# Second, casting transfer for the rounded part of each weight piece, in place of ScalarE's rounding

## What is computed

```python
for l in range(DEPTH):
    h = h + 0.5 * swiglu(rmsnorm(h, ffn1_norm[l]), ffn1_w_gu[l], ffn1_w_down[l])
    h = h + mixer(rmsnorm(h, mix_norm[l]), w_in[l], ret_gn[l], w_ret_proj[l],
                  w_sb_proj[l], w_out[l], pos, valid)
    h = h + 0.5 * swiglu(rmsnorm(h, ffn2_norm[l]), ffn2_w_gu[l], ffn2_w_down[l])
```

## Time and profile before

| what | value |
|---|---|
| median of 3 runs | 1291.62 us (1291.59 to 1291.71) |
| the profiled execution, whole | 1291.65 us |
| its span, first to last instruction | 1289.8 us |
| granted TensorE clock, mean | 0.999 |
| weight transfers on SP's queue | 407 of 512 KB and two halves |
| read from HBM | 217.04 MB, 169 GB/s over the span |

### The profile page before, as it was taken

How to read it: one execution, slowest core, us unless ns; L and a number is a source line. 1 busy time by engine, 2 the same in 40 slices (tenths; PEclk the granted TensorE clock), 3 DMA queues, 4 the chain that set the end, 5 groups by cost and what they waited for, 6 DMA issues and landing times.

```text
span 1289.8 us, 26118 instructions
## 1 busy us (share of the span) xinstructions
PE 1281.2 (99%) x10298; PEld 1276.1 (99%) x10298; DVE 866.0 (67%) x1078; ACT 697.2 (54%) x932; POOL 54.2 (4%) x48
## 2 busy tenths in 40 slices
PE   8999999999999999999999999999999999999998
PEld 8999999999999999999999999999999999999998
DVE  7766556878876776665476665568788777766653
ACT  6544445757766554444454444457578665544442
POOL 2000001000000010000010000010000000100000
PEclk9999999999999999999999999999999999999999
DMA  7655554544344455555545555555544445555552
GB/s 293 198 178 178 178 169 160 180 166 146 118 142 144 160 187 178 167 179 180 172 157 194 170 171 180 176 168 180 166 145 131 138 158 179 196 185 182 187 179 83
DMA packets 60705, 219.30 MB, mean 170 GB/s; under 512 B 6864, under 2 KB 6992, under 8 KB 60496
## 3 DMA queue, kind: packets, MB, share of 16 engines
q1 hardware_dynamic: 60048, 217.01, 50.6%
q10 hardware_dynamic: 576, 1.11, 0.3%
HBM read 217.04 MB, written 1.05 MB: 169 GB/s over the span
## 4 chain that ended last, share of the span: by engine, by line
PE 98%; DVE 1%; ACT 1%; DMA 0%; issue 0%; ACTq 0%
PE bank L1102 31%; PE bank L1104 31%; PE bank L1103 31%; PE bank L1246 1%; PE bank L1337 1%; PE bank L1366 1%; PE bank L1235 1%; PE bank L1218 0%; DMA raw<-stream 0%; PE bank L1253 0%; PE bank L1057 0%; PE bank L1116 0%; DVE w_lo L656 0%; PE bank L1061 0%; PE bank L1059 0%; PE bank L1236 0%
## 5 line engine op out<-in xcount | busy, mean ns | idle before, releaser
L656 DVE TENSOR_TENSOR w_lo<-raw,w_hi 128x1024 fp32r<-128x1024 f32 x407 | 508.8, 1256 | 270.5 <-ACT w_hi L406 265.7
L1102 PE MATMUL bank<-xh,w_hi 128*128 128x272 f32 (+1 forms) x2224 | 642.6, 289 | 0.1
L406 ACT ACTIVATE w_hi<-raw 128x1024 fp32r<-128x1024 f32 x407 | 428.3, 1058 | 391.8 <-PE bank L1104 391.0
L1104 PE MATMUL bank<-xh,w_lo 128*128 128x272 f32 (+1 forms) x2224 | 635.8, 286 | 0.0
L1103 PE MATMUL bank<-xl,w_hi 128*128 128x272 f32 (+1 forms) x2224 | 635.5, 286 | 0.0
L1103 PEld LDWEIGHTS bank<-xl,w_hi 128*128 128x128 f32 x2224 | 418.6, 188 | 0.2
L1102 PEld LDWEIGHTS bank<-xh,w_hi 128*128 128x128 f32 x2224 | 418.3, 188 | 0.5 <-DVE w_lo L656 0.3
L1104 PEld LDWEIGHTS bank<-xh,w_lo 128*128 128x128 f32 x2224 | 418.1, 188 | 0.0
L1104 PE MATMUL bank<-gh,w_lo 128*128 128x272 f32 (+1 forms) x1016 | 290.9, 286 | 0.0
L1102 PE MATMUL bank<-gh,w_hi 128*128 128x272 f32 (+1 forms) x1016 | 290.7, 286 | 0.0
L1103 PE MATMUL bank<-gl,w_hi 128*128 128x272 f32 (+1 forms) x1016 | 289.8, 285 | 0.0
(11 more groups left out here) (197 smaller groups left out, 731.3 us busy)
## 6 DMA issues: line engine op xcount, KB each, us to landing
raw<-stream SPq DMA_DIRECT2D x407, 512.0 KB, 3.3
table<-tables SPq DMA_DIRECT2D x1, 1424.0 KB, 7.8
gain_h<-tokens SPq DMA_DIRECT2D x2, 272.0 KB, 6.2
raw<-stream SPq DMA_DIRECT2D x2, 256.0 KB, 4.5
out<-rv_gb ACTq DMA_DIRECT2D x2, 256.0 KB, 2.8
out<-rv_gb SPq DMA_DIRECT2D x2, 256.0 KB, 2.7
rv_gb<-squares SPq DMA_DIRECT2D x1, 384.0 KB, 8.0
gain_h<-tokens ACTq DMA_DIRECT2D x1, 300.0 KB, 4.2
```

The lines of the kernel that those rows point to most:

```text
L406: eng.activation(w_hi[:, slot, :], raw[:, slot, :], ACT.Copy).then_inc(hi_ready, 1)
L656: eng.tensor_tensor(w_lo[:, slot, :], raw[:, slot, :], w_hi[:, slot, :].bitcast(F32), ALU.subtract).then_inc(lo_ready, 1)
L1102: pe.matmul(out, wh, hi, start=first, stop=False)
L1104: mm = pe.matmul(out, wl, hi, start=False, stop=last)
```

## The change

Pieces 4 to 407 get their w_hi by a second transfer of the same 512 KB from HBM, which casts from float32 to fp32r on the way. POOL's queue issues it (`cast_hi`), after a wait for the piece that used the slot before. ACT's roundings of these pieces go away; those of the first four stay. DVE's `split_lo` now waits for both transfers of its piece. POOL's additions and copies are placed at fixed steps between the issues: POOL's program has the same loops as the others. In the rotary part, where ACT relied on split_hi's wait, it now has one of its own.

```diff
+        hi_in = [sem(f"hi_in{i}") for i in range(RING)]
...
+            def cast_hi(n, slot):
+
+                pool.wait_ge(piece_done, n - (RING - 1))
+                pool.dma_start(w_hi[:, slot, :], stream[n]).then_inc(hi_in[slot], 16)
+
+            def squares_after(rnd, p):
+
+                if p:
+                    add_squares(rnd, p)
+                if p == PAIRS - 1:
+                    join_squares(rnd)
+
+            def join_squares(rnd):
+                pool.wait_ge(ssq_added, rnd * ADDS + ADDS)
+                pool.tensor_tensor(ssq[:, 0, :], ssq[:, 0, :], ssq[:, 1, :], ALU.add).then_inc(ssq_joined, 1)
+
+            def ffn(l, f):
...
+                for j in range(4):
+                    cast_hi(base + (j + RING), (off + j) % RING)
+                    if base == 0 and j < ADDS:
+                        add_squares(0, j + 1)
...
+                with pool.Fori(1, ITERS) as it:
+                    for j in range(4):
+                        cast_hi(base + it * 4 + (j + RING), (off + j) % RING)
+                for q in range(QUADS):
+                    for c in range(ITERS):
+                        s = GU + q * ITERS + c
+                        if not last or s + RING < FFN:
+                            cast_hi(base + (s + RING), (off + s) % RING)
+                        if c >= ITERS - 2 and not last:
+                            squares_after(l * 3 + 2 * f + 1, 2 * q + c - (ITERS - 2))
+
+            def mixer(l):
+                base = l * PER_LAYER + FFN
+                for s in range(MIX):
+                    cast_hi(base + (s + RING), (FFN + s) % RING)
+                    if s == 2 * U_V + 1:
+                        place_first_keys(l)
+                    if s == 2 * U_SK + 4:
+                        place_second_keys(l)
+                    if s == 2 * U_SQ[1] + 1:
+                        place_last_queries(l)
+                    if s >= S_OUT and s % 2:
+                        squares_after(l * 3 + 2, (s - S_OUT) // 2)
...
                 with eng.Fori(1, ITERS) as it:
-                    for j in range(4):
-                        split_hi(base + it * 4 + (j + RING), (off + j) % RING)
-                        if j == 1:
-                            silu(it)
+                    silu(it)
                     hidden_hi(it)
...
                     if s % 2 and u < U_V:
 
                         q0 = first_kept(u, qf)
+                        eng.wait_ge(piece_done, base + (s + 1))
...
-            def split_lo(n, slot):
-
-                eng.wait_ge(hi_ready, n + 1)
+            def split_lo(n, slot, first=False):
+
+                if first:
+                    eng.wait_ge(hi_ready, n + 1)
+                else:
+                    eng.wait_ge(hi_in[slot], (n - slot) * (16 // RING))
+                    eng.wait_ge(raw_ready[slot], (n - slot) * (16 // RING) + 16)
                 eng.tensor_tensor(w_lo[:, slot, :], raw[:, slot, :], w_hi[:, slot, :].bitcast(F32),
                                   ALU.subtract).then_inc(lo_ready, 1)
```

More of the change, by code:

```diff
@@ L350, in add_squares @@
                 pool.tensor_tensor(ssq[:, :, :], ssq[:, :, :], squares_home(rnd, p), ALU.add).then_inc(ssq_added, 1)
-            def layer(l):
[L353 to L359, removed]
+            def cast_hi(n, slot):
+                pool.wait_ge(piece_done, n - (RING - 1))
+                pool.dma_start(w_hi[:, slot, :], stream[n]).then_inc(hi_in[slot], 16)
@@ new lines, in squares_after @@
+            def squares_after(rnd, p):
[7 more added lines that the diff above has]
+            def ffn(l, f):
+                off = 0 if f == 0 else FFN + MIX
+                base = l * PER_LAYER + off
+                last = first_query(l) > 0 and f == 1
+                for j in range(4):
+                    cast_hi(base + (j + RING), (off + j) % RING)
+                    if base == 0 and j < ADDS:
+                        add_squares(0, j + 1)
+                if base == 0:
+                    join_squares(0)
+                with pool.Fori(1, ITERS) as it:
[8 more added lines that the diff above has]
+                            squares_after(l * 3 + 2 * f + 1, 2 * q + c - (ITERS - 2))
@@ L361, in place_keys @@
+            def layer(l):
+                ffn(l, 0)
+                mixer(l)
+                ffn(l, 1)
             def place_keys(keys):
@@ L369, in place_tail_queries, with place_first_keys @@
                 mm.then_inc(placed, 1)
-            def place_queries(l):
+            def place_first_keys(l):
                 pool.wait_ge(ssum_done, l * 3 + 2)
@@ L377, in place_queries, with place_second_keys @@
                 pool.wait_ge(rq_tail_in, l + 1)
+            def place_second_keys(l):
                 pool.wait_ge(ret_tail_scores, l + 1)
@@ L381, in place_queries, with place_last_queries @@
                 pool.wait_ge(key_tail_ready, 2 * l + 2)
+            def place_last_queries(l):
                 pool.wait_ge(unit_evicted, evicted(l, U_SQ[1]))
@@ L399, in raw_count, with split_hi @@
                 return (n - slot) * (16 // RING) + 16
-            def split_hi(n, slot, first=False):
-                if not first:
-                    eng.wait_ge(piece_done, n - (RING - 1))
+            def split_hi(n, slot):
                 eng.wait_ge(raw_ready[slot], raw_count(n, slot))
@@ L456, in ffn @@
                         eng.preload_act_table_set("silu_and_others")
-                    split_hi(base + (j + RING), (off + j) % RING)
                 silu(0)
@@ L471, in ffn @@
                             take_h(l * 3 + 2 * f + 1, 2 * q + c - (ITERS - 2), q0, final=last)
-                        if not last or s + RING < FFN:
-                            split_hi(base + (s + RING), (off + s) % RING)
             def mixer(l):
@@ L480, in mixer @@
                         take_h(l * 3 + 2, (s - S_OUT) // 2, qf)
-                    split_hi(base + (s + RING), (FFN + s) % RING)
                     u = s // 2
@@ L628, in _ @@
             hi_of_h(0, 1, 0)
-            split_hi(1, 1, first=True)
+            split_hi(1, 1)
             eng.wait_ge(h_loaded[2], 16)
@@ L633, in _ @@
             hi_of_h(0, 3, 0)
-            split_hi(2, 2, first=True)
+            split_hi(2, 2)
             squares_of_h(0, 0, 0)
             squares_of_h(0, 1, 0)
-            split_hi(3, 3, first=True)
+            split_hi(3, 3)
             squares_of_h(0, 2, 0)
@@ L1016, in _ @@
             lo_of_h(0, 1, 0)
-            split_lo(1, 1)
+            split_lo(1, 1, first=True)
             eng.wait_ge(h_loaded[2], 16)
@@ L1021, in _ @@
             lo_of_h(0, 3, 0)
-            split_lo(2, 2)
-            split_lo(3, 3)
+            split_lo(2, 2, first=True)
+            split_lo(3, 3, first=True)
             eng.wait_ge(squares_in, 32)
```

## The result

The changed kernel takes 1525.97 us (median of 4 runs, 1520.25 to 1533.02), the one before 1291.63: 234 us more, a ratio of 1.182 (95% interval 1.179 to 1.185). The direction was forecast, and so was what happens in retention and stick-breaking. The size was not: the forecast was 97 us more, and 1526 lies in the range only because of its upper end.

The account below looks back on a forecast made before the run. PE, busy 99% of the span, was taken to bound the kernel. Terms of 43 + 38 + 8 + 3 + 5 = 97 us on the profiled 1291.65 us gave 1389 us, range 1325 to 1590.

Parts of the forecast that it names:

- Retention and stick-breaking: PE stalls in the mixer: retention L - 1.8, 16 times, 43 us; stick-breaking L - 2.1, 16 times, 38 us.
- L: Time from E to the landing of w_hi, before which DVE's w_lo cannot start.
- The price of L: Casting transfer on POOL's queue: 3.3 us from SP's median plus about 1.2, so 4.5; ends 3.0 and 7.7.
- E: End of the weight piece PE has just finished, when a slot of the ring comes free.
- Values and merges: Stalls of L - 3.2 for three value units in 2 layers, 8 us; last merge before output projection, 3 us.
- DMA engines: Two transfers a piece want 348 GB/s against 409 to 412 at the start, 85 to 91% full: no cost.
- Feed-forward: nothing: In the feed-forward, DVE has w_lo at 5.7 us and PE needs it at 9.0: no cost until L passes 7.8.
- POOL's order: At five stage ends and the start, transfers go out late behind POOL's additions: 5 us.
- Rival A: DMA engines become the bound, casting taking them twice as long in all pieces: 1590 us, chance 0.16.
- Rival B: POOL's issue waits for DVE's instruction under way, L 5.7: 1441 us; chance 0.17 with other causes of longer L.
- Rival C: w_hi lands within 1.8 us of E, so no PE chain is late: 1287 us, chance 0.02.
- Rival D: Nothing changes, needing L near 1.8 or a scheduler letting DVE pass w_lo; chance of no change 0.03.

Follow-up runs that it names:

- raw once: The changed kernel with SP loading raw of the first four pieces only, so half the bytes with the same waits for w_hi: 1396.75 us, ratio 1.081.

## Why the prediction was wrong in size

- **Retention and stick-breaking: right, the waits and their size.** L - 1.8 and L - 2.1 hold to 0.2 us at the places shown (3.66 for 3.5, 1.83 for 1.83). The 16 waits before L1384 (L1337 of the old numbering) came to 40.9 us, forecast 43; before L1282 (the old L1235) there were 12 waits with 32.8 us, forecast 16 with 38. The stages grew by 107, and the part beyond the waits is mostly the clock.
- **The price of L: right where it was used, too low elsewhere.** It was 4.4 in the mean at the heads, for 4.5, and partly by luck: "3.3 plus about 1.2" is made up otherwise. The issue goes out 0.3 us after E, the software queue adds 0.3 to the landing (3.6 for 3.3), and the rest is the second stream, which varies with the stage. In the feed-forwards w_hi landed in 6.3 us, and in the whole kernel in 5.4.
- **Values and merges, "8" and "3": too low.** PE waited 12 us at the values for the eviction (L1265, 5 times), 3 more behind the tails, and 11 in the merges (L1149 behind L910 and L904).
- **DMA engines, "nothing": the step that failed.** It took 409 to 412 GB/s from the program's start as what the engines can do, and 85 to 91% as their load. That rate belongs to many transfers under way. In the feed-forward some 4 are under way, and the queues moved 338 of the 348 wanted, at a share of 0.97. The rows of the feed-forward itself, 174 GB/s at a share of 0.53, give 328 at a share of 1, which would have been a warning. No more than that: the same working gives 327 for one plain transfer under way (157 at 0.48), and four moved 397. The second stream cost 81 us by itself and part of the 49. That also undid "Feed-forward: nothing", whose condition, L under 7.8, held in the median: the rate, and not the cover of one piece, set the pace.
- **The limit of 358 GB/s.** The Trainium skill ("DMA: Bandwidth & Descriptors", Where 436 GB/s comes from) gives about 358 GB/s for each core. I had let rows 10 decide against it, rightly as a limit, since eight transfers under way move 408 here. The best stretch of the changed kernel, 1400 to 1430 us, has 362. The rates fit the number under way; nothing here shows a fixed limit at 358.
- **POOL's order, "5 us": too low.** The additions one transfer later gave back 21 us. The forecast compared 6.8 with 7.8 us of cover. In the first down projections w_hi lands in 6.1 us, L is 6.4, and with the 2.3 of the late issue that is 8.7, past it.
- **Missing: the clock.** Behind some of PE's waits it was granted its lower level for a while. Some 66 us of the 83 of additional busy time in the changed kernel are its part, by the mean clock, more than a quarter of the 234; in the run that has no such waits there is next to none (1281.9 us busy, clock 0.999). The runs don't separate this term from the waits; it goes with them. What the other 17 us are stays open.
- **Rival A** (a casting transfer takes the engines twice as long) fell: with the same number under way, casting ones moved 10 to 12% less. **Rival B** (DVE holds POOL up) fell: the issue took 527 to 528 ns from minimum to median beside a busy DVE and went out 0.3 us after E in the median, and with raw once the transfer landed in 3.6 us. **Rival C** needed an L of 1.8; the least landing time was 3.4. **Rival D** (no change) fell with the 234 us.

## What to carry to other kernels

Before doubling a stream, count how many transfers will be under way in the stage concerned, and take the rate from a row with that number; a burst elsewhere in the program, with more of them, does not give it. Look at L where each chain uses it: a median over the whole kernel hid that the heads had 3.6 us to landing and the feed-forwards 6.3. When a producer's wait gets longer, look at what stands behind it in the same engine's order: here moving one instruction by one step gave back 125 of 234 us, and cost nothing in the kernel before. Taking work off an engine that PE isn't waiting for gained nothing here, and what took its place cost.

## What the runs showed that I had not expected

Two transfers of 512 KB under way on one queue moved 255 GB/s and four 397. A cast from float32 to fp32r on POOL's queue landed in the same 3.6 us as a plain transfer there, and POOL was busy 0.53 us for its issue. The clock fell behind single waits of 2.11 to 3.66 us at retention: 0.56 granted in the 6 us after the longest, with the blocks 0.68 instead of 0.38 us apart. The runs of the changed kernel spread over 13 us, those of the kernel before over 1.
